# Expert stages of a hybrid model on one core: gathered and output rows as half rows on 128 partitions, transposes moved, block loops grouped

## The chip, the core and the metric

The kernel runs on one core of a Trainium2 chip. A core has TensorE (PE, matrix products and transposes into PSUM), VectorE (DVE), ScalarE (ACT), GpSimd (POOL) and SyncE (SP), and 16 DMA engines that move data between HBM and the core's SBUF. The metric is the device time of one execution in microseconds. All values are float32.

## The reference

`reference()` is two blocks. The first is a convolution module and a retention module on 512 tokens of width 1024. The second has two layers, each with windowed attention, local mixers, and a hierarchical mixture of experts. The mixture is the part that the change touches:

```python
N_EXPERTS, TOP_K, D_EXPERT = 32, 2, 512          # d_model 1024
expert = g_idx * EXP_PER_GROUP + e_idx           # two experts of one group for each token
...
xs = h[slot_tok].reshape(n_blocks, MOE_BLOCK, d_)
def run(args):
    xb, e = args
    return (jax.nn.silu(xb @ w1[e]) * (xb @ w3[e])) @ w2[e]
ys = lax.map(run, (xs, block_e)).reshape(-1, d_)
return jnp.zeros_like(h).at[slot_tok].add(ys * slot_gate[:, None])
```

Layer 0 routes 768 tokens (512 and a context of 256), layer 1 routes 512. Each expert has w1 and w3 of 1024x512 and w2 of 512x1024, 2 MiB each, so a layer reads 192 MiB of expert weights.

## The kernel before

The kernel is written by hand for each engine: every engine has its own instruction stream, and semaphores order them. Nothing reschedules them.

In an expert stage the tokens of each expert are packed into blocks of 64 slots (`SB`). The experts with even numbers form stream 0, those with odd numbers stream 1. A step `i` handles block `i` of stream 0 and then block `i` of stream 1 (`rounds`, L397). Each stream has one set of weight buffers (`m_w`), one of row buffers and four PSUM banks.

For block `i` of stream `s` TensorE runs `expert_step` (L1278): `products` (L1241: 8 k-steps, each with a product for w1 and one for w3, 64 columns of the array each, side by side, into one bank), then `turn_hidden` for block i-1 (L1254: four transposes of the gated hidden rows), `turn_rows` for block i+1 (L1230: eight transposes of the gathered rows, 64 partitions by 128), and `outputs` for block i-1 (L1265: w2, both halves of the columns side by side).

Around it, ScalarE applies SiLU (L854) and copies half of the output rows (L847). VectorE copies the transposed rows (L1895) and hidden rows (L1903) to SBUF, multiplies by the gate (L1921) and copies the other half of the output (L1911). GpSimd gathers the rows of block i+1 (indirect DMA, L2034, 64 rows of 4 KiB onto 64 partitions) and scatters those of block i-2 (L2050). SP loads the weights (`load_step`, L584, DMA at L575): w1 and w3 of block i+1 once `products` of block i of the same stream is done, w2 of block i once `outputs` of block i-1 is done. If block i+1 has the same expert as block i, a register makes the load a no-op.

The number of blocks is known only at run time. A fixed loop runs steps 2 to 15; a second loop (L405) runs over all remaining possible steps, 24 in layer 0 and 16 in layer 1, and each round asks whether `i <= last` (L406). `last` is the same for both streams: the longer one's last block. Every engine runs this loop.

Before the stage, products of one-hot matrices (L1218) turn the routing into slot lists: for each block the token rows and the gates, together in 128 output partitions. After the stage, the output rows are read back from HBM (L608) and the layer norm finishes on VectorE (L1950 to L1952).

## Time and profile before

| what | value |
|---|---|
| time, median of 3 runs (lowest to highest) | 3241.57 us (3236.73 to 3242.39) |
| the profiled execution's own time | 3238.72 us |
| its span, first to last instruction | 3236.9 us |
| TensorE busy | 2784.1 us (86%) |
| VectorE busy | 1128.3 us (35%) |
| DMA moved | 602.90 MB, 186 GB/s over the span |
| L1250 (`products`), x2688 | 658.5 us busy, 646 ns mean |
| L1273 (`outputs`), x1344 | 310.2 us busy, 603 ns mean |
| SiLU calls, L854 | x84 |

The page is one execution. Busy time of TensorE counts overlapping matmuls once. The 84 calls of L854 are the blocks that were computed in both layers, 42 steps of two streams. In the trace the first expert stage lies at about 1564 to 2175 us and the second at about 2544 to 3196 us. The granted clock (PEclk) is given as a share of full speed: 1.0 is 2.4 GHz, 0.5 is 1.2 GHz.

### The profile page before, as it was taken

The numbers are of one execution on the slowest core, as the hardware profiler recorded it, in microseconds if no ns is written. First come the engines' busy times: TensorE is split into PE (matmuls) and PEld (weight loads), VectorE is DVE, ScalarE is ACT, GpSimd is POOL, SyncE is SP. The second block draws the span as 40 slices with busy tenths as digits, with TensorE's granted clock in tenths as the row PEclk, the third lists the DMA queues.
The fourth block names the chain that finished last, engine by engine and source line by source line (L and its number), as shares of the span: only waits on it lengthen the run. The fifth ranks groups of instructions, "written<-read, shape, count | busy, mean of one in ns | idle before, by whom it ended". The sixth has DMA issues, their size and how long they took to land.

```text
span 3236.9 us, 33858 instructions
## 1 busy us (share of the span) xinstructions
PE 2784.1 (86%) x11728; PEld 1295.0 (40%) x11728; DVE 1128.3 (35%) x2173; ACT 458.6 (14%) x848; POOL 304.7 (9%) x432
## 2 busy tenths in 40 slices
PE   6999969999999999899698877866999679997783
PEld 3444424444444455555333322323564323332221
DVE  3998960320011232544511111127254411211114
ACT  2111131100110102521000000001151000100000
POOL 0101011000000000001211111110000211111110
PEclk9999989999999999998799989987989699998987
DMA  6655521222211201012699999974101798489994
GB/s 209 209 194 182 169 91 54 94 78 78 78 52 50 91 26 52 1 41 104 223 334 320 387 386 384 347 269 154 52 1 60 268 385 288 128 300 392 387 359 171
DMA packets 270442, 602.90 MB, mean 186 GB/s; under 512 B 18016, under 2 KB 42912, under 8 KB 268960
## 3 DMA queue, kind: packets, MB, share of 16 engines
q1 hardware_dynamic: 255584, 580.70, 49.8%
q0 software_dynamic: 14784, 21.21, 2.2%
q8 instruction: 47, 0.77, 0.1%
q14 instruction: 27, 0.22, 0.0%
HBM read 739.11 MB, written 29.46 MB: 237 GB/s over the span
## 4 chain that ended last, share of the span: by engine, by line
PE 70%; DMA 17%; DVE 6%; issue 3%; ACT 2%; SPq 1%; POOL 0%; DVEq 0%; POOLq 0%; ACTq 0%
DMA arena<-in_w 16%; PE psum L1250 14%; PE psum L916 10%; PE psum L965 10%; PE psum L1093 9%; PE psum L937 7%; PE psum L1188 4%; PE psum L1273 4%; PE psum L1140 2%; PE psum L1129 2%; PE psum L901 1%; SPq L575 1%; PE psum L986 1%; PE psum L1203 1%; PE psum L1152 1%
## 5 line engine op out<-in xcount | busy, mean ns | idle before, releaser
L1250 PE MATMUL psum<-arena 128*64 128x512 f32 x2688 | 658.5, 646 | 167.9 <-DMA arena<-in_w 123.4
L1250 PEld LDWEIGHTS psum<-arena 128*64 128x64 f32 x2688 | 221.2, 148 | 594.7 <-issue 549.3
L916 PE MATMUL psum<-arena 128*128 128x512 f32 x768 | 345.4, 603 | 2.8 <-ACT arena L647 2.8
L965 PE MATMUL psum<-arena 128*128 128x512 f32 x768 | 329.9, 592 | 0.8 <-ACT arena L639 0.8
L1273 PE MATMUL psum<-arena 128*64 128x512 f32 x1344 | 310.2, 603 | 16.6 <-DVE arena L1903 12.2
L1349 DVE SCALAR_TENSOR_TENSOR arena<-arena 128x512 f32<-128x512 f32 x464 | 308.7, 744 | 0.0
L1903 DVE COPY arena<-psum 128x256 f32<-128x256 f32 x84 | 35.5, 424 | 763.3 <-PE psum L1261 756.6
L1093 PE MATMUL psum<-arena 128*128 128x512 f32 (+1 forms) x800 | 288.3, 522 | 5.9 <-issue 4.0
L937 PE MATMUL psum<-arena 128*128 128x512 f32 x512 | 225.3, 603 | 11.1 <-POOL arena L1996 10.4
L965 PEld LDWEIGHTS psum<-arena 128*128 128x128 f32 x768 | 145.8, 190 | 184.2 <-issue 183.2
L916 PEld LDWEIGHTS psum<-arena 128*128 128x128 f32 x768 | 143.1, 191 | 175.0 <-issue 175.0
L1093 PEld LDWEIGHTS psum<-arena 128*128 128x128 f32 x800 | 152.9, 192 | 134.4 <-issue 124.7
L1273 PEld LDWEIGHTS psum<-arena 128*64 128x64 f32 x1344 | 100.1, 138 | 165.7 <-issue 165.7
L854 ACT ACTIVATE arena<-psum 64x512 f32<-64x512 f32 x84 | 49.9, 595 | 781.9 <-PE psum L1250 781.9
L937 PEld LDWEIGHTS psum<-arena 128*128 128x128 f32 x512 | 99.0, 194 | 137.1 <-issue 135.9
L1188 PE MATMUL psum<-arena 128*128 128x512 f32 x320 | 137.9, 593 | 3.3 <-ACT arena L803 3.3
L1911 DVE COPY arena<-psum 64x512 f32<-64x512 f32 x84 | 58.2, 693 | 219.4 <-PE psum L1273 219.4
L2011 POOL TENSOR_TENSOR arena<-arena 128x1024 f32<-128x1024 f32 x10 | 27.4, 2756 | 871.7 <-DVE arena L1517 871.7
L847 ACT ACTIVATE arena<-psum 64x512 f32<-64x512 f32 x84 | 49.6, 590 | 369.2 <-PE psum L1273 369.2
L2034 POOL DMA_INDIRECT arena<-moe_in,arena x88 | 91.4, 1039 | 78.9 <-POOL arena L2031 72.3
L2050 POOL DMA_INDIRECT moe_out<-arena x76 | 72.4, 952 | 235.6 <-DVE arena L1911 235.6
L1140 PE MATMUL psum<-arena 128*128 128x128 f32 x640 | 86.5, 287 | 9.4 <-issue 4.8
(268 smaller groups left out, 2144.9 us busy)
## 6 DMA issues: line engine op xcount, KB each, us to landing
arena<-in_w SPq DMA_DIRECT2D x260, 2048.0 KB
arena<-in_w_ada SPq DMA_DIRECT2D x48, 1024.0 KB, 5.2
arena<-in_conv_w_in SPq DMA_DIRECT2D x24, 1024.0 KB
arena<-in_ret_w_in SPq DMA_DIRECT2D x12, 2048.0 KB, 7.8
arena<-in_w_in SPq DMA_DIRECT2D x8, 2048.0 KB, 8.2
arena<-moe_out SPq DMA_DIRECT2D x10, 1024.0 KB, 9.0
arena<-in_conv_w_out SPq DMA_DIRECT2D x4, 2048.0 KB, 10.2
arena<-in_ret_w_out SPq DMA_DIRECT2D x4, 2048.0 KB, 7.9
```

The costliest lines, as they stand in the source:

```text
L916: m = pe.matmul(bank(b + c), w[:, k, c * P:(c + 1) * P], c_hT[:, k, :], start=(k == 0), stop=(k == KD - 1))
L937: m = pe.matmul(bank(2 * t + hf), mem(y + S * k + P * t, P), slot_rows(n)[:, k % 4, hf * CW:(hf + 1) * CW], start=(k == 0), stop=(k == KI ...
L965: m = pe.matmul(bank(4 * (n % 2) + j), l_, r_, start=(k == 0), stop=(k == KD - 1))
L1093: m = pe.matmul(o, l_, r_, start=(k == 0), stop=(k == KD - 1))
L1129: m = pe.matmul(psum[:, at:at + P * len(ts)], q, b_kT[part, h // 4, ts[0] * P:(ts[-1] + 1) * P], start=True, stop=True)
L1140: m = pe.matmul(bank(4 + kv, P, hh * P), b_sb[i % 2][:, 4 * kv + hh, c * P:(c + 1) * P], b_dg[i % 2][:, 4 * kv + hh, :], start=True, stop= ...
L1188: m = pe.matmul(bank(2 * (t % 4) + hf), y[:, t * P:(t + 1) * P], slot_rows(base + 4 + k // 4)[:, k % 4, hf * CW:(hf + 1) * CW], start=(k = ...
L1250: m = pe.matmul(bank(4 * s)[part], m_xsT[s][:, k, :], m_w[s][j][:, k, :], start=(k == 0), stop=(k == KD - 1))
L1273: m = pe.matmul(bank(4 * s + 3)[SB * hf:SB * hf + SB], m_hT[s][:, k, :], m_w[s][2][:, k, hf * CW:(hf + 1) * CW], start=(k == 0), stop=(k = ...
L1349: ins = dve.scalar_tensor_tensor(out=acc, in0=u, scalar=w[:, j:j + 1], in1=acc, op0=ALU.mult, op1=ALU.add)
L2034: pool.indirect_dma_start(out=m_xs[s], in_=moe_in[l], out_offset=None, in_offset=bass.IndirectOffsetOnAxis(m_gi[s], 0), bounds_check=nt * ...
L2050: pool.indirect_dma_start(out=moe_out[l], in_=m_y[s], in_offset=None, out_offset=bass.IndirectOffsetOnAxis(m_si[s], 0), bounds_check=2 * n ...
```

## The change

It has these parts.

1. **Half rows.** The HBM tensors of gathered and output rows are seen as rows of 512. One gather of a block brings 128 half rows of 2 KiB onto 128 partitions: partition p holds the first half of slot p's row, partition 64+p the second. The scatter writes 128 half rows. `m_xs` and `m_y` become 128x512. The rows' index lists have 128 entries per block, and the product that makes them (L1218) becomes two products, one for each half of the partitions; the gates get a product of their own.
2. **Four transposes.** `turn_rows` turns 128x128 tiles, four instead of eight per block.
3. **One bank pair per stream.** The transposed rows share a bank with the products of w1 and w3, and the transposed hidden rows share one with the outputs. `turn_rows` now waits until the gate multiplication has read the bank. `turn_hidden` moves into the middle of `products`, and `outputs` comes directly behind `products`, ahead of `turn_rows`.
4. **Copies.** The output rows need one ScalarE copy of 128x512 in place of one on ScalarE and one on VectorE. SiLU writes where the gate multiplication then works in place.
5. **Own last block per stream, in groups.** The second loop runs over groups of five steps; a group is skipped as a whole, and inside it each block of each stream has its own condition. Layer 0 has 5 groups, layer 1 has 4.
6. **Lookahead.** At the start of a stage only the rows of stream 0's first block are turned before the first product. The layer norm's scaling of residual rows (`complete_rows`) is put into two portions of six operations (layer 0) in place of four of three. w1 and w3 of a stream share one semaphore.

The core of the diff:

```diff
-            with eng.Fori(E // 2, NBS[l]) as i:
-                with eng.If(i <= last[0]):
-                    for s in range(2):
-                        step(s, i, first)
+            with eng.Fori(0, (NBS[l] - E // NS) // GROUP) as g:
+                with eng.If(g * GROUP + E // NS <= last[NS]):
+                    for j in range(GROUP):
+                        for s in range(NS):
+                            with eng.If(g * GROUP + (E // NS + j) <= last[s]):
+                                step(s, g * GROUP + (E // NS + j), first)
...
-                        m = pe.matmul(bank(6, nr), posw[:, j, :], blk[:, j, :], start=(j == 0), stop=(j == 2 * nt - 1))
+                        for hf in range(2):
+                            m = pe.matmul(bank(6, nr)[SB * hf:SB * hf + SB], row[:, j, :], blk[:, j, :],
+                                          start=(j == 0), stop=(j == 2 * nt - 1))
...
                     pe.wait_ge(moe(l, s, "gather"), count(l, s, "gather", 16 * i + 16))
                     if early >= 1:
-                        pe.wait_ge(moe(l, s, "rows"), count(l, s, "rows", i))
+                        pe.wait_ge(moe(l, s, "hidden"), count(l, s, "hidden", i))
                     pe.sem_inc(sem("settled"), 1)
-                    for k in range(KD):
-                        m = pe.transpose(bank(4 * s + 1, SB, SB * k), m_xs[s][:, k * P:(k + 1) * P],
-                                         ident[0:SB, 0:SB])
+                    for k in range(KD // 2):
+                        m = pe.transpose(bank(2 * s, P, P * k), m_xs[s][:, k * P:(k + 1) * P], ident)
...
                     for k in range(KD):
+                        at = P * (k % 4) + SB * (k // 4)
+                        if k == KD // 2 and early >= 1:
+                            turn_hidden(s, i - 1, early - 1)
...
                     products(s, i, early)
                     if early >= 1:
-                        turn_hidden(s, i - 1, early - 1)
+                        outputs(s, i - 1, early - 1)
+                    elif s + 1 < NS:
+                        turn_rows(s + 1, 0, 0)
                     turn_rows(s, i + 1, early + 1)
-                    if early >= 1:
-                        outputs(s, i - 1, early - 1)
-
-                for s in range(2):
-                    turn_rows(s, 0, 0)
+
+                turn_rows(0, 0, 0)
...
-                    act.activation(m_y[s][:, 0:CW], bank(4 * s + 3)[0:SB], ACT.Copy).then_inc(moe(l, s, "y"), 1)
+                    act.activation(m_y[s], bank(2 * s + 1), ACT.Copy).then_inc(moe(l, s, "y"), 1)
...
-                    pool.indirect_dma_start(out=m_xs[s], in_=moe_in[l], out_offset=None,
+                    pool.indirect_dma_start(out=m_xs[s], in_=halves_in, out_offset=None,
                                             in_offset=bass.IndirectOffsetOnAxis(m_gi[s], 0),
-                                            bounds_check=nt * P - 1, oob_is_err=False)\
+                                            bounds_check=2 * nt * P - 1, oob_is_err=False)\
```

The order of the instructions on TensorE in the fixed loop of layer 1, one block, before (products, hidden rows, gathered rows, outputs):

```order
L1250 MATMUL psum<-arena 64x512 x16
L1261 MATMUL psum<-arena 128x64 x4
L1232 ISA
L1237 MATMUL psum<-arena 128x64 x8
L1267 ISA
L1268 REGISTER_ALU
L1270 ISA
L1273 MATMUL psum<-arena 64x512 x8
```

and after the change (products L1295, hidden rows L1306, outputs L1317, gathered rows L1282):

```order
L1295 MATMUL psum<-arena 64x512 x8
L1301 REGISTER_ALU
L1303 REGISTER_ALU
L1306 MATMUL psum<-arena 128x64 x4
L1295 MATMUL psum<-arena 64x512 x8
L1312 ISA
L1313 REGISTER_ALU
L1317 MATMUL psum<-arena 64x512 x8
L1277 ISA
L1279 REGISTER_ALU
L1282 MATMUL psum<-arena 128x128 x4
```

The transposes of the hidden rows now split the products into two runs of eight, and the outputs follow without a transpose between. The other stream's block follows in the same order.

The second loop of layer 1 on TensorE, before, with its body of two blocks left out:

```order
L405 UNCONDITIONAL_BRANCH
L405 ISA
L406 COMPARE_AND_BRANCH
...
L406 UNCONDITIONAL_BRANCH
L405 REGISTER_ALU
L405 COMPARE_AND_BRANCH
```

and after the change, with the bodies left out:

```order
L436 UNCONDITIONAL_BRANCH
L436 ISA
L437 COMPARE_AND_BRANCH
L440 REGISTER_ALU
L440 COMPARE_AND_BRANCH
...
L440 UNCONDITIONAL_BRANCH
L440 REGISTER_ALU
L440 COMPARE_AND_BRANCH
...
L440 UNCONDITIONAL_BRANCH
L436 REGISTER_ALU
L436 COMPARE_AND_BRANCH
```

A skipped round took two branches for one step; now it takes two for five steps, and each block that is reached has a branch of its own.

The start of layer 1's expert stage on TensorE, before:

```order
L1237 MATMUL psum<-arena 128x64 x16
L1250 MATMUL psum<-arena 64x512 x16
L1237 MATMUL psum<-arena 128x64 x8
L1250 MATMUL psum<-arena 64x512 x16
L1237 MATMUL psum<-arena 128x64 x8
L1250 MATMUL psum<-arena 64x512 x16
L1261 MATMUL psum<-arena 128x64 x4
L1237 MATMUL psum<-arena 128x64 x8
L1273 MATMUL psum<-arena 64x512 x8
```

and after the change:

```order
L1282 MATMUL psum<-arena 128x128 x4
L1295 MATMUL psum<-arena 64x512 x16
L1282 MATMUL psum<-arena 128x128 x8
L1295 MATMUL psum<-arena 64x512 x16
L1282 MATMUL psum<-arena 128x128 x4
L1295 MATMUL psum<-arena 64x512 x8
L1306 MATMUL psum<-arena 128x64 x4
L1295 MATMUL psum<-arena 64x512 x8
L1317 MATMUL psum<-arena 64x512 x8
```

The second stream's rows are turned behind the first product and not ahead of it.

## Rows read from the trace of the kernel before

**Rows 1.** Windows of the two expert stages; columns as the first line says.
```profile
core 0: us, PE busy (x) PEld busy (x) DVE busy (x) ACT busy (x) POOL busy (x), PEclk, DMA share, GB/s
1668.00:1732.00 64.00, 61.39 (x328) 24.83 (x328) 14.04 (x23) 6.26 (x11) 12.69 (x23) 1.00 0.89 306
2113.00:2148.00 35.00, 34.04 (x180) 13.68 (x176) 7.18 (x12) 3.48 (x6) 3.69 (x8) 1.00 0.78 289
2692.00:2790.00 98.00, 92.81 (x480) 36.17 (x478) 19.57 (x32) 9.36 (x16) 18.16 (x32) 0.98 0.72 243
2790.00:2855.00 65.00, 64.00 (x342) 25.96 (x340) 14.67 (x24) 7.11 (x12) 12.87 (x24) 1.00 0.21 59
1803.00:2014.00 211.00, 163.84 (x760) 61.37 (x761) 29.46 (x48) 14.63 (x25) 27.24 (x48) 0.89 1.04 386
```

**Rows 2.** Chain in order of time (start us, us, what), two blocks bound by TensorE.
```profile
2783.61 6.87 PE psum L1250 x32
2790.48 0.39 PE psum L1261 x4
2790.87 0.50 PE psum L1237 x8
2791.38 0.15 issue
2791.52 3.65 PE psum L1273 x16
2802.56 0.43 DVE arena L1903
```

**Rows 3.** The same view, end of the first expert stage.
```profile
2143.80 3.65 PE psum L1273 x16
2147.45 11.72 issue
2160.63 9.36 PE psum L1273 x32
```

**Rows 4.** Line L406: branches of the skipping loop on TensorE's queue.
```profile
L406 PEldq COMPARE_BRANCH  x40: 73/213/215, 2031.4 to 3178.3; - x40
```

**Rows 5.** Chain, before the router: transposes of 128x128.
```profile
1510.82 1.75 PE psum L1027 x8
1512.57 3.26 PE psum L1203 x16
```

**Rows 6.** Page, part 5: SiLU on ScalarE.
```profile
L854 ACT ACTIVATE arena<-psum 64x512 f32<-64x512 f32 x84 | 49.9, 595 | 781.9 <-PE psum L1250 781.9
```

**Rows 7.** Chain at the second stage's first weight load.
```profile
2559.62 8.39 DMA arena<-in_w
2568.02 5.58 issue
```

**Rows 8.** Chain, end of the second expert stage.
```profile
3146.86 0.39 PE psum L1261 x4
3163.15 6.87 PE psum L1250 x32
```

**Rows 9.** Timeline, end of the second stage (start us, us, engine, line, operation).
```profile
3182.82 8.54 PE L1273 MATMUL psum<-arena 128*64 128x512 f32 x32 [2.66 <-DVE arena L1903]
```

**Rows 10.** Timeline, start of the first expert stage.
```profile
1582.22 1.21 DVE L1933 TENSOR_TENSOR arena<-arena 128x1024 f32<-128x1024 f32 x1
```

**Rows 11.** Page, part 3: the indirect DMAs' queue (packets, MB, share).
```profile
q0 software_dynamic: 14784, 21.21, 2.2%
```

**Rows 12.** Indirect DMAs' queue in 1563 to 1580 us.
```profile
q0 software_dynamic: 320, 0.86, 18.1%
```

**Rows 13.** Page, part 5: the gathers' issue on GpSimd.
```profile
L2034 POOL DMA_INDIRECT arena<-moe_in,arena x88 | 91.4, 1039 | 78.9 <-POOL arena L2031 72.3
```

**Rows 14.** Lines L916 and L901, the program's first loop, four rounds.
```profile
L916 PE MATMUL psum<-arena x768: 592/592/1192, 32.5 to 421.6; 128*128 128x512 f32 x192
L901 PE MATMUL psum<-arena x1536: 272/273/298, 42.6 to 423.0; 128*32 128x128 f32 x192
```

More of the change, by code:

```diff
@@ L45 @@
 SB = 64
+NS = 2
+EPN = -(-E // NS)
+GROUP = 5
 NO_ROW = 4096
@@ L381, in build @@
-        REUSED0 = [
-            {"index": ("ra_ms", 4), "turned": ("ri_mm", 48), "rows": ("ri_dve", 16)},
-            {"index": ("ra_sd", 4), "turned": ("ri_act", 32), "rows": ("ra_sc", 16)}]
+        MOE_SEMS = ("w13", "w2", "gather", "scatter", "index", "turned", "rows", "product", "silu", "hidden",
+                    "hid_t", "hid_rows", "out", "y")
+        U = T + TX
+        reused_hw = [("const_in", 32), ("ctx_in", 32), ("fg_in", 16), ("x_in", 16 * TX), ("cv_w0", 192), ("cv_w1", 192)]
@@ new lines, in build @@
+        reused_late += [("kT", 2 * T), ("kt", 2 * T), ("at_o", 4 * U), ("ob_x", 2 * U), ("ob_mm", 2 * U), ("lg_mm", U),
+                        ("upad", 2), ("rt_M", 2), ("rt_act", 4), ("rt_dve", 4), ("at_l", AH * U), ("at_s", AH * U),
+                        ("at_p", AH * U), ("at_e", (AH + 1) * U)]
+        REUSED = [{}, {}]
+        for s_ in range(NS):
+            for what_ in MOE_SEMS:
+                if what_ in ("w13", "w2"):
+                    REUSED[1][s_, what_] = reused_hw.pop()
+                elif what_ in ("gather", "scatter"):
+                    if reused_pool:
+                        REUSED[1][s_, what_] = reused_pool.pop()
+                else:
+                    REUSED[1][s_, what_] = reused_late.pop() if reused_late else reused_old.pop()
@@ L385, in shared @@
+        for s_ in range(NS):
+            for what_ in MOE_SEMS[4:]:
+                if reused_old:
+                    REUSED[0][s_, what_] = reused_old.pop()
         def shared(l, s, what):
-            return (REUSED if l else REUSED0)[s].get(what, (f"m{s}_{what}", 0))
+            return REUSED[l].get((s, what), (f"m{s}_{what}" if what in MOE_SEMS[:2] or l == 0 else f"n{s}_{what}", 0))
         def moe(l, s, what):
@@ L567, in _ @@
                 sp.wait_ge(sem("hx2_out"), past("hx2_out", l) + 16 * nt)
-                for j, what in enumerate(("w1", "w3", "w2")):
-                    sp.dma_start(m_w[1][j], ws[j][:, kk[j]:2 * kk[j], :]).then_inc(moe(l, 1, what), 16)
+                for j in range(3):
+                    first_weights(1, j)
                 sp.wait_ge(sem("meta"), past("meta", l) + 1)
@@ L1213, in _ @@
                 nr = NR[l]
-                posw, blk = mem3(g_posw, 2 * nt, 2 * SB), mem3(g_blk, 2 * nt, nr)
+                row, wgt, blk = (mem3(o, 2 * nt, n) for o, n in ((g_row, SB), (g_wgt, SB), (g_blk, nr)))
                 for k in range(2):
@@ L1223, in _ @@
                                      ident[0:nr, 0:nr])
+                m.then_inc(sem("rank"), 1)
+                for j in range(2 * nt):
+                    m = pe.matmul(bank(5, nr, 256)[0:SB], wgt[:, j, :], blk[:, j, :], start=(j == 0),
+                                  stop=(j == 2 * nt - 1))
                 m.then_inc(sem("rank"), 1)
@@ L2015, in _ @@
                 pool.wait_ge(sem("hx_in"), past("hx_in", l) + nt)
-                for s in range(2):
+                for s in range(NS):
                     link(pool.memset(m_xs[s], 0.0))
@@ L2061, in _ @@
-                for s in range(2):
-                    gather(s, 0, 0)
+                    gather(s, i + 2, early + 2, 2 * i + 2 if early >= 1 else 3)
+                    if early >= 1:
+                        scatter(s, i - 1, early - 1, 2 * i + 3)
+                for s in range(NS):
+                    gather(s, 0, 0, 1)
+                for s in range(NS):
+                    gather(s, 1, 1, 2)
                 pool.wait_ge(sem("meta"), past("meta", l) + 1)
                 last = last_blocks(pool, l)
-                rounds(pool, l, last, move_step, first=3)
@@ L2079, in _ @@
-                for s in range(2):
+                rounds(pool, l, last, move_step)
+                for s in range(NS):
+                    scatter(s, last[s], 1, 2 * last[s] + 4)
+                for s in range(NS):
                     pool.wait_ge(moe(l, s, "scatter"), count(l, s, "scatter", 16 * last[s] + 16))
                     settled()
-                    pool.wait_ge(moe(l, s, "gather"), count(l, s, "gather", 16 * last[s] + 32))
+                    pool.wait_ge(moe(l, s, "gather"), count(l, s, "gather", 16 * last[s] + 48))
```

280 lines of the change are left out of this document (132 added, 148 removed).

## The prediction

> **What bounds the kernel now.** Only the two expert stages change, so I read them alone, by stretches. The windows [rows 1] show two regimes. From 1803 to 2014 us the DMA engines are full (share 1.04, 386 GB/s) while TensorE is busy 164 of 211 us: there a step of two blocks waits for its weights, and nothing that TensorE does faster or slower counts. In four other stretches TensorE is busy 95 to 98% of the time and the DMA share is 0.89, 0.78, 0.72 and 0.21: the blocks there reuse an expert's weights, and TensorE sets the pace. They last 64 + 35 + 98 + 65 = 262 us. The chain of waits in one of them [rows 2] gives the block: 6.87 us products, 0.39 us four hidden transposes, 0.50 us eight row transposes, 0.15 us until the outputs start, 3.65 us outputs, 11.56 us in all. So the 262 us hold about 22.6 blocks. Every second block also has VectorE's copy of the hidden rows (0.43 us, the last of rows 2) on the path, which takes the place of the row transposes and costs about the same.
>
> The third thing to see is idle time at the ends. In the first stage TensorE finishes block 18's outputs at 2143.80 + 3.65 = 2147.45 us and then does nothing for 11.72 us [rows 3]: 20 rounds of the second loop are skipped, 0.586 us each. A branch on its queue takes 213 ns [rows 4], and a skipped round has two. The outputs of the last blocks then take 9.36 us, at a clock that has fallen, for what takes 2 x 3.65 at 2.4 GHz.
>
> **The change part by part.** Which blocks exist follows from the inputs: with the reference's routing the streams have 20 and 20 blocks in layer 0 and 21 and 22 in layer 1. The kernel before computes 2 x 20 + 2 x 22 = 84, the changed one 83.
>
> *The block on TensorE.* The three transposing pieces cost 0.39 + 0.50 + 0.15 = 1.04 us for 12 transposes of 64-partition tiles. The eight alone take 0.50, so 0.0625 us each, and 12 x 0.0625 = 0.75; the other 0.29 us are two changes of tile shape, from the products' 128x64 tiles to the transposes' and back. After the change four transposes stand inside the products: 0.25 + 0.29 = 0.54 us. The four row transposes are 128x128. Eight of these took 1.75 us [rows 5], so four take 0.88, with two more changes of shape 1.17 us. Together 1.71 in place of 1.04, or +0.67; VectorE's copy no longer waited for gives back some 0.1. I take +0.55 us a block. The lowest this can be is -0.3 (transposes of 128x128 at the price of two small ones, and no cost at the extra changes of shape, since rows 5 show none between two groups of 128x128 tiles), the highest +1.0 (the whole 0.29 at each of two extra changes, and 0.22 us a transpose). The new wait, `turn_rows` for the gate multiplication, is hidden: SiLU takes 595 ns [rows 6], the multiplication works on a tile of the same size, and the outputs, 3.65 us, lie in front.
> 22 blocks x 0.55 = +12 us (bounds -7 and +22).
> The Trainium skill, TensorEngine Tiling (Array Packing), Key Properties, says that changing the tiling mode, and not just the tile, drains TensorE. The 0.15 us between the last transpose and the outputs [rows 2] agrees. By that rule four changes a block in place of two would be the larger part of the loss, and the sum would stay as it stands; what it speaks against is the lower bound.
>
> *End of the first stage.* The outputs of block 18 end about 0.5 us earlier (outputs before row transposes, one insertion more), at 2147. Skipping costs four groups of 0.586 and two single branches with their arithmetic, 0.3 each: 2.9 us. The last hidden transposes follow to about 2151.5. w2 of the last block is issued when block 18's outputs end. From issue to the next product a fresh pair w1, w3 took 8.39 + 5.58 = 14.0 us [rows 7]; 4.2 MB at 386 GB/s are 10.9 of these, so w2 with half the bytes takes 14.0 - 5.4 = 8.6 us, until 2155.6. Stream 0's outputs run before, stream 1's until 2159.3, against 2169.99 before. -10.5 us. What is late next is w2's load. Bounds: -12 (clock up, load quicker) and -3 (a branch inside a group as dear as a whole round).
>
> *End of the second stage.* Block 21 of stream 0 goes, 11.56 us of TensorE, but its expert's neighbour is waited for: w1 and w3 of block 21 of stream 1 are issued when product (1,20) ends, at 3146.86 [rows 8], and land 14.0 us later at 3160.9, against a product that started at 3163.15. So only 2 us come of the block that is gone. The product then ends at 3168.9, the outputs of block 20 at 3172.5, w2 lands 8.6 us later at 3181.1, and the last outputs end at 3184.8, against 3182.82 + 8.54 = 3191.36 [rows 8, 9]. -6, after half a microsecond for the lower clock. Bounds -9 and -2. The skipping (eight single branches, two groups, 3.6 us in place of 10 rounds) lies beside the load.
>
> *Start of a stage.* One row turn and the wait for the second gather leave the path to the first product, -1.3 us in each layer. Against that the second product waits for the gate multiplication and then for the row turns (+2.1), and in layer 0 VectorE's six scalings in a row, 1.2 us each [rows 10], hold back a hidden copy (+2). The split products for the slot lists run as side-by-side halves, 24 pairs, at about the time of 24 whole ones. Together +0.5 for both layers, bounds -3 and +6 (the pairs not side by side: twice 5.4 us in layer 0, partly beside VectorE).
>
> *Indirect DMAs.* The queue took 2.2% of the span for 21.21 MB [rows 11], 71 us of all 16 engines. In 1563 to 1580 us it shows 320 packets with 0.86 MB in 18.1% of 17 us x 16 [rows 12], so 0.86 MB are about 210 rows of 4 KiB at 230 ns, and the rest are unused slots and completions. The bytes stay, the rows double. If the half row costs half, nothing changes; if each adds 20 ns, 5120 more rows are 6 us of all engines, and half of the stages' time is full. GpSimd's issue took 1039 ns for 64 rows [rows 13]; 128 may take up to twice that, which is beside TensorE's 11.6 us except for the first gather and the last scatter of a stage. I take +1 (bounds -4 and +7).
>
> Sum: +12 - 10.5 - 6 + 0.5 + 1 = -3 us. The profiled execution took 3238.72 us (span 3236.9), so 3235.7; that execution lies 2.85 us under the median of 3241.57, and I set the time against the median: 3238.6, say 3239.
>
> **The rivals.**
> *The transposes cost nothing on the path.* For it: the queue of weight loads in front of a block in the 0.89 and 0.78 stretches absorbs a late product, and rows 5 show no pause at a change of instruction. Against: 0.21 in the 65 us stretch, where nothing absorbs. The 12 us fall to 0 or below: 3239 - 13 = 3226.
> *The block costs 1.0 us more or TensorE counts in more blocks.* For it: rows 2 show every gap on the chain, and the product that starts when its weights land is also 0.54 us longer, which in a stretch that is nearly full delays the next load. 32 blocks x 0.95 = 30 us in place of 12: 3239 + 18 = 3257, slower than before. It decides from about 0.7 us a block in 22 blocks, or 0.55 in 29. Against: in the full stretches TensorE has 47 us of idle time in 12 or 13 blocks, nearly 4 us each.
> *The groups' code must be fetched again.* A group on TensorE is ten blocks of 60 pairs of weight load and matmul, 1200 instructions and some 150 others. If it did not stay loaded, each of the six skipped groups would wait for code twice, at 2 to 3 us: about 30 us, of which the w2 loads hide half: 3239 + 15 = 3254. Against: the first loop of the program has (768 + 1536) / 4 = 576 pairs a round [rows 14], 1152 instructions, and it runs on from 32.5 to 423 us with matmuls of 592 and 272 ns and no wait on code that I can see. The Trainium skill, Runtime: NRT & Kernel Launch, Instruction fetch mechanics, gives TensorE 2048 instructions of memory and the other engines 512; by it TensorE's group would fit. On the others a group is some 230 instructions or fewer.
> *The change does not do what it says*, that is, the end wait stays since another engine leaves the loop later: VectorE left it last in layer 1 (the last outputs waited 2.66 us for its copy [rows 9]). The ends would give -8 in place of -16.5: 3247.
>
> **How the numbers follow.** Forecast, 3239 with its own range 3230 to 3248: 0.45. Transposes free, 3226: 0.2. Dear blocks, 3257: 0.17. Code fetched again: 0.06. Ends half won: 0.12. A measurement of this kernel can tell about 0.2%, 6.5 us, from no change: faster is below 3235, slower above 3248. The forecast's 0.45 splits 0.14, 0.28, 0.03; the second gives 0.18 faster and 0.02 same; the third and fourth 0.21 slower and 0.02 same; the last 0.07 same, 0.05 slower. Faster 0.32, same 0.39, slower 0.29. The range 3225 to 3257 leaves 0.2 out.
>
> **What the profile after would show.** Right: blocks of 12.0 to 12.3 us in the stretch that reuses weights in layer 1, with row transposes of 0.9 us; no 11.72 us of idle TensorE in layer 0 but 3 to 5; 83 SiLU calls; in layer 1 a wait for weights ahead of the last product; the same 34 us steps where the DMA share is 1.04. Wrong: a block of 11.5 us or less, or above 12.6; steps in the full stretches that change by more than 0.5 us, which would put the half rows in the DMA engines at fault; idle TensorE at a branch in the middle of the second loop.

## The result

| | before | after |
|---|---|---|
| median | 3239.32 us (3236.73 to 3242.39, 4 runs) | 3218.06 us (3211.45 to 3222.34, 4 runs) |
| profiled execution, span | 3238.72, 3236.9 us | 3222.34, 3220.5 us |

The ratio of the times is 0.9932, with a 95% interval of 0.991 to 0.9954: 21 us faster, below the predicted range (3225 to 3257). The profiled execution is the slowest of the four, so its trace shows 16 us of the 21.

**The pace of TensorE.** The chain of waits in the stretch of layer 1 that reuses weights ([rows 2] show the same for before; L1306 are the hidden rows' transposes, L1295 the products, L1317 the outputs, L1282 the gathered rows' transposes):

```profile
2764.51 0.39 PE psum L1306 x4
2764.90 3.58 PE psum L1295 x16
2768.49 3.43 PE psum L1317 x16
2771.92 0.59 PE psum L1282 x4
2772.51 3.58 PE psum L1295 x16
2776.09 0.39 PE psum L1306 x4
```

From one set of hidden transposes (L1306) to the next are 11.58 us, against 11.56 before. No pause stands between the pieces. Four transposes of 128x128 (L1282) take 0.59 us.

**The full stretch**, with the columns of rows 1 (TensorE busy, its weight loads, VectorE, ScalarE, GpSimd, granted clock, DMA share, GB/s):

```profile
1803.00:2014.00 211.00, 169.55 (x728) 59.23 (x724) 24.08 (x39) 15.49 (x26) 29.62 (x49) 0.90 1.04 393
```

The DMA share is 1.04 as before, but 393 GB/s are moved in place of 386 [rows 1]. From the end of the first product to the end of the last, layer 0 takes 557.6 us against 562.6 before, layer 1 takes 606.0 against 610.7, the latter with a block fewer. (Here and below, where a time is given from the end of a product without a row, the end is read from the start of the SiLU that waits for it, 0.13 us later.)

**The end of layer 0.** The chain, without its short pieces:

```profile
2132.45 3.58 PE psum L1295 x16
2136.03 3.43 PE psum L1317 x16
2139.46 0.60 PE psum L1282 x4
...
2144.02 0.43 DVE arena L1950
2144.59 8.62 PE psum L1317 x32
```

The last outputs end at 2153.21 us, 17.18 us after the last product. Before, that was 27.14 us, 11.72 of them idle [rows 3]. Between the row transposes (L1282) and VectorE's copy (L1950) are 4 us, nearly all of them VectorE's own branches. TensorE was out of the loop earlier: it is idle for 2.16 us and has ended the last hidden transposes at 2143.04 us.

**The end of layer 1.** The last product ends at 3147.14 us. What follows on the chain is SP's queue (SPq), which no row of before shows:

```profile
3143.56 3.58 PE psum L1295 x16
3147.14 3.46 PE psum L1317 x15
3150.92 0.39 SPq L615
...
3153.16 4.45 issue
3157.74 3.54 issue
3161.35 2.23 issue
3163.62 2.94 issue
3166.70 2.83 issue
3169.60 2.00 issue
3171.64 2.98 issue
3174.82 0.36 SPq L571
...
3176.77 7.48 DMA arena<-moe_out
3184.37 1.24 DVE arena L1987
```

L615 at 3150.92 us is SP's last load of weights, L571 its first one behind the loop. Between them SP has nothing to wait for, and yet it leaves the loop only at 3174.82 us. TensorE's last outputs had ended at 3165.6 us, 18.4 us after the last product. From the last product to the first operation on the output rows (L1987) are 37.2 us, against 30.7 before.

Page, part 3 and part 5: the indirect DMAs' queue, queue 14, which carries instructions (27 packets before), and SiLU, 83 calls in place of 84:

```profile
q0 software_dynamic: 14944, 21.23, 1.9%
q14 instruction: 51, 0.41, 0.0%
L893 ACT ACTIVATE arena<-psum 64x512 f32<-64x512 f32 x83 | 49.3, 595 | 875.2 <-PE psum L1295 875.2
```

### The profile page after: what moved, and what is told of

The parts are those of the page before. It is cut to its first block, busy times and chain, and to the rows that moved or that the text cites. A ratio compares the mean times of both kernels' runs of the same rounds, so it can differ in the third digit from the quotient of the medians.

```text
span 3220.5 us, 33096 instructions
## 1 busy us (share of the span) xinstructions
PE 2781.2 (86%) x11400; PEld 1265.5 (39%) x11400; DVE 1076.8 (33%) x2088; ACT 458.2 (14%) x846; POOL 315.7 (10%) x436
## 4 chain that ended last, share of the span: by engine, by line
PE 69%; DMA 19%; DVE 6%; issue 3%; ACT 2%; SPq 1%; POOL 0%; DVEq 0%; POOLq 0%; ACTq 0%
DMA arena<-in_w 18%; PE psum L1295 14%; PE psum L955 10%; PE psum L1004 10%; PE psum L1132 9%; PE psum L976 7%; PE psum L1227 4%; PE psum L1317 3%; PE psum L1179 2%; PE psum L1168 2%; PE psum L940 1%; PE psum L1025 1%; PE psum L1242 1%; SPq L615 1%; PE psum L1191 1%
## 5 line engine op out<-in xcount | busy, mean ns | idle before, releaser
L1295 PE MATMUL psum<-arena 128*64 128x512 f32 x2656 | 672.9, 653 | 169.2 <-DMA arena<-in_w 167.4
L1295 PEld LDWEIGHTS psum<-arena 128*64 128x64 f32 x2656 | 205.0, 148 | 515.7 <-issue 510.4
L1317 PE MATMUL psum<-arena 128*64 128x512 f32 x1328 | 303.3, 600 | 3.6 <-DVE arena L1950 2.8
L1950 DVE COPY arena<-psum 128x256 f32<-128x256 f32 x83 | 35.1, 424 | 490.9 <-PE psum L1306 484.6
L893 ACT ACTIVATE arena<-psum 64x512 f32<-64x512 f32 x83 | 49.3, 595 | 875.2 <-PE psum L1295 875.2
L1317 PEld LDWEIGHTS psum<-arena 128*64 128x64 f32 x1328 | 97.0, 139 | 195.2 <-issue 195.2
L1960 DVE SCALAR_TENSOR_TENSOR arena<-arena,psum 64x512 f32<-64x512 f32 x83 | 61.3, 739 | 327.4 <-ACT arena L893 327.4
L1943 DVE COPY arena<-psum 128x512 f32<-128x512 f32 x87 | 60.1, 691 | 211.9 <-PE psum L1282 211.9
L2070 POOL COPY arena<-arena 128x1 int32 (+1 forms) x91 | 17.8, 196 | 878.8 <-PE psum L1282 837.5
L1179 PE MATMUL psum<-arena 128*128 128x128 f32 x640 | 86.5, 287 | 9.4 <-issue 4.8
## 6 DMA issues: line engine op xcount, KB each, us to landing
arena<-moe_out SPq DMA_DIRECT2D x10, 1024.0 KB, 10.5
```

Source lines behind the costliest of these rows:

```text
L1179: m = pe.matmul(bank(4 + kv, P, hh * P), b_sb[i % 2][:, 4 * kv + hh, c * P:(c + 1) * P], b_dg[i % 2][:, 4 * kv + hh, :], start=True, stop= ...
L1295: m = pe.matmul(bank(2 * s)[part], m_xsT[s][:, at:at + SB], m_w[s][j][:, k, :], start=(k == 0), stop=(k == KD - 1))
L1317: m = pe.matmul(bank(2 * s + 1)[SB * hf:SB * hf + SB], m_hT[s][:, k, :], m_w[s][2][:, k, hf * CW:(hf + 1) * CW], start=(k == 0), stop=(k = ...
L1960: dve.scalar_tensor_tensor(out=m_h[s], in0=m_h[s], scalar=gate, in1=bank(2 * s)[0:SB], op0=ALU.mult, op1=ALU.mult).then_inc(moe(l, s, "hid ...
```

## The experiments

All times are medians. The kernels of one group ran beside the kernel before on the same chip. The ratios are to it.

### First group: what does SP cost, and which half rows pay?

**The changed kernel again.** No edit.

> The changed kernel as it is, for comparison with the three kernels run beside it. Both theories: 0.993 of the kernel before, about 3218 us, with steps of 33.2 us in the stretch of layer 1 where the DMA engines are full, and 7 us in the trace's chain of waits on SP between the last outputs of layer 1 and the reading of the output rows.

Measured: 3216.99 us (3214.54 to 3218.88), ratio 0.9934 (0.9921 to 0.9946). SP is ready (it issues L571, its first load behind the loop) 27.7 us after the last product of layer 1, and the read of the output rows is issued at 29.45 us.

**SP in single steps.**

```diff
-                rounds(sp, l, last, load_step)
+                rounds(sp, l, last, load_step, group=1)
```

> SP alone runs the second loop in single steps (as the kernel before did), the other engines keep groups of five. Theory: in layer 1 SP leaves its last group late, because each jump over a block that is left out lands on instructions that must be fetched (waits of 2 to 4.5 us each in the changed kernel's chain from 3151 to 3175 us); a single step stays loaded. The reading of the output rows then starts at the landing of the last scatter, about 7 us earlier than now: 3211 us, 0.998 of the changed kernel, with no SP issue on the chain there. Rival: SP is not late by itself but ends when the last scatter and the signal for it arrive, or what GpSimd does is as late: same time as the changed kernel within 2 us, the chain there then shows GpSimd. A second rival: single steps cost SP two branches for each of 14 skipped rounds, 0.3 to 0.6 us each, so 4 to 8 us, and nothing is won.

Measured: 3208.6 us, ratio 0.9904 (0.989 to 0.9919). SP is ready 11.47 us after the last product, and the read is issued at 21.15 us, at the landing of the last scatter:

```profile
3166.26 2.27 DMA moe_out<-arena
...
3168.84 5.68 DMA arena<-moe_out
```

The theory's main claim holds: 8 us of SP's late exit were on the path. In layer 0 the single steps cost something. SP takes 10.5 us there for 22 rounds (2135.0 to 2145.5 us) in place of 2.9 for five, issues the loads behind the loop later, and the last scatter lands after 6.85 us in place of 2.62. That the scatter is slow because of these loads is argued, not shown.

**Gathers of whole rows**, on 64 partitions:

```diff
-        m_xs = [mem(W0 + 12288 + 512 * s, CW) for s in range(NS)]
+        m_xs = [mem(W0 + 2048 + D * s, D, SB) for s in range(NS)]
...
-                    for k in range(KD // 2):
-                        m = pe.transpose(bank(2 * s, P, P * k), m_xs[s][:, k * P:(k + 1) * P], ident)
+                    for k in range(KD):
+                        m = pe.transpose(bank(2 * s, SB, SB * k), m_xs[s][:, k * P:(k + 1) * P],
+                                         ident[0:SB, 0:SB])
```

> Only the gathers go back to whole rows of 4 KiB on 64 partitions, with eight transposes of 64x128 a block; the scatters stay half rows. Theory one (the gathered half rows on 128 partitions load the DMA engines less): the steps in the full stretch of layer 1 go back from 33.2 to 33.7 us, and the time rises by 8 to 10 us over both layers, to 3227 us. Theory two (the scatters do it, or the order of the products does): steps stay at 33.2 us and the time stays within 3 us of the changed kernel's. On the block bound by TensorE both say the same: the transposes take 0.50 us and their change 0.15 us in place of 0.59, so 22 blocks are 0 to 2 us longer.

Measured: 3243.06 us, ratio 1.0013 (1.0005 to 1.0022). It is theory one, but 26 us and not 8 to 10. The block bound by TensorE is 11.63 us. The rest stands in the windows of the full stretches, of this kernel:

```profile
1850.00:2000.00 150.00, 118.81 (x530) 42.52 (x532) 16.01 (x26) 10.12 (x17) 19.32 (x33) 0.89 1.04 386
```

and of the changed kernel:

```profile
1850.00:2000.00 150.00, 118.26 (x506) 42.00 (x504) 16.71 (x27) 10.72 (x18) 22.01 (x36) 0.91 1.04 393
```

In the stretches ahead of it the steps are longer too. From the end of the first product to that of the seventh this kernel takes 73.15 us in layer 0, the changed kernel 67.92 and 69.17 in its two profiled executions (this group's and that of the result); in layer 1 these are 85.18 against 82.42 and 83.00.

**Scatters of whole rows**, from 64 partitions:

```diff
-                    act.activation(m_y[s], bank(2 * s + 1), ACT.Copy).then_inc(moe(l, s, "y"), 1)
+                    for hf in range(2):
+                        act.activation(m_y[s][:, CW * hf:CW * (hf + 1)], bank(2 * s + 1)[SB * hf:SB * (hf + 1)], ACT.Copy)\
+                            .then_inc(moe(l, s, "y"), 1)
```

> Only the scatters go back to whole rows of 4 KiB from 64 partitions (two ScalarE copies of 64x512 a block in place of one of 128x512); the gathers stay half rows. Theory one (the gathers make the full steps shorter): steps stay at 33.2 us, the time within 3 us of the changed kernel's. Theory two (the scatters do): steps of 33.7 us, 8 to 10 us longer. If neither this kernel nor the one with whole gathers moves the steps, the half rows are not the cause and the order of TensorE's work is. Both: the last copy of a stage is 0.6 us later on ScalarE, twice, 1 us.

Measured: 3215.15 us, ratio 0.9934 (0.992 to 0.9948), 394 GB/s in the same window. The scatters' shape is worth nothing that the runs can tell.

### Second group: length or partitions, and the parts of the order

**Half rows, two gathers onto the same 64 partitions** (the second with `element_offset=CW`, transposes as with whole rows):

```diff
+                    for hf in range(2):
+                        pool.indirect_dma_start(out=m_xs[s][:, CW * hf:CW * (hf + 1)], in_=halves_in, out_offset=None,
+                                                in_offset=bass.IndirectOffsetOnAxis(m_gi[s], 0),
+                                                element_offset=CW * hf,
```

> The rows are gathered as half rows of 2 KiB, but onto 64 partitions: two gathers of 64 half rows a block, side by side in the free dimension, and eight transposes of 64x128, as in the kernel with whole gathers. Theory one (what costs is the length of the row: 4 KiB pieces among the weights' own of about 2 KiB): as the changed kernel, 3217 us, steps of 33.5 us in the full stretch, and 388 to 393 GB/s there. Theory two (what costs is that all rows land on 64 of the 128 partitions): as the kernel with whole gathers, 3243 us, steps of 34 us or more, 359 to 386 GB/s in stretches whose DMA share is over 1. Both: GpSimd has one issue of 1 us more a block, which is beside the 11.6 us of a block.

Measured: 3248.46 us, ratio 1.0028 (1.0019 to 1.0038). Theory two, and 5 us more than with whole rows, with twice the issues. Halving the row's length wins nothing as long as the rows land on 64 partitions. The DMA view of 2058 to 2085 us gives GB/s in 40 slices of 0.675 us. The changed kernel (first group), the one with whole gathers, and this one:

```profile
GB/s 416 395 407 388 388 385 382 388 388 388 385 391 385 383 352 385 388 380 401 382 388 385 385 385 388 391 391 410 407 401 419 413 413 397 343 391 401 394 391 404
```

```profile
GB/s 404 373 397 361 206 231 234 294 370 404 407 401 413 394 428 413 407 401 385 419 279 282 361 400 410 385 413 388 388 388 388 388 388 385 385 382 388 385 388 388
```

```profile
GB/s 385 391 267 325 261 246 346 407 380 416 413 400 401 425 407 413 382 388 401 264 397 276 370 388 397 404 401 407 379 388 388 388 388 385 382 391 382 388 385 385
```

In the second and third the rate falls to 206 to 330 GB/s for some four slices at a time, with the engines counted as busy throughout; in the first it never leaves 343 to 419. The stretches 1850 to 1877, 1900 to 1927 and 1950 to 1977 us say the same: there the slices of the kernel before and of these two fall to 212 to 325 GB/s again and again, those of the changed kernel never below 361. Over the four slices 206, 231, 234, 294 the loss against 388 is about 1 us. That one kernel has the dips and the other has not is shown; why they arise is not. The Trainium skill, SBUF — State Buffer, Door 1: The DMA port swizzle, says that partitions 0 to 63 reach only 8 of the 16 ports by which DMA writes SBUF. The trace agrees in the dips to nearly half of 388. No run here tried other sets of 64 partitions, and in the kernels with the dips the gathered rows also lie at another address within a partition than in the changed one; no run moved them alone. Reading from 64 partitions (the scatters above) showed nothing of the kind.

**Hidden rows turned behind the products:**

```diff
-                        if k == KD // 2 and early >= 1:
-                            turn_hidden(s, i - 1, early - 1)
...
                     if early >= 1:
+                        turn_hidden(s, i - 1, early - 1)
                         outputs(s, i - 1, early - 1)
```

> The transposes of the hidden rows stand behind the sixteen product pairs, ahead of the outputs, and not in their middle; all else as changed. Theory: the insertion costs nothing and hides VectorE's copy of the hidden rows (0.43 us) and TensorE's wait for it. Without it the outputs wait: a block bound by TensorE grows from 11.58 to about 12.0 us, 22 blocks are 10 us, 3227 us in all. Rival (my prediction's: each change of instruction shape costs 0.15 us, and the insertion brings two more): the block shrinks by 0.3 and grows by 0.43, so it stays within 0.15 us and the time within 3 us. In the full stretches both say no change: 33.5 us steps.

Measured: 3223.31 us, ratio 0.9949 (0.9934 to 0.9964), 5 to 6 us more than the changed kernel. The chain in the stretch that reuses weights:

```profile
2763.86 0.39 PE psum L1304 x4
2764.25 0.56 issue
2764.81 3.65 PE psum L1315 x16
2768.47 0.59 PE psum L1282 x4
2769.05 7.02 PE psum L1293 x32
2776.07 0.40 PE psum L1304 x4
```

A block is 12.21 us, as the theory said and more than the rival allowed: 0.56 us of waiting for VectorE's copy come back. The two changes of shape that the insertion brings cost 7.16 - 7.02 = 0.14 us together at most, and the copy that it hides is four times that. The time rises by half of the theory's 10 us: from the first product to the last, layer 1 is 7.2 us longer than in the changed kernel of the first group (611.87 against 604.69), layer 0 no longer (550.43 against 550.92).

**The common last block:**

```diff
-            return [eng.value_load(g_n[l][0:1, s:s + 1], min_val=E // NS - 2, max_val=NBS[l] - 2) + 1
-                    for s in range(NS + 1)]
+            v = eng.value_load(g_n[l][0:1, NS:NS + 1], min_val=E // NS - 2, max_val=NBS[l] - 2) + 1
+            return [v] * (NS + 1)
```

> Both streams again run to the last block of the longer one, groups of five kept. Layer 0 has 20 and 20 blocks and does not change. In layer 1 block 21 of stream 0 is computed again (84 blocks). Theory: of its 11.56 us of TensorE nearly all lies beside the load of w1 and w3 of the other stream's block 21, as in the kernel before, so 0 to +3 us: 3218 us. Rival: the block's own load of 6 MB (a gathered block without rows has an expert too) or its place ahead of the last block puts 10 us or more on the path: 3228 us.

Measured: 3205.77 us (3203.43 to 3206.29), ratio 0.9891 (0.9873 to 0.9909). Neither theory said that: 11 us faster with one block more. Block 21 itself costs little: from the end of layer 1's first product to the end of its last are 607.39 us, against 604.69 and 605.99 in the changed kernel's two profiled executions. These 1.4 to 2.7 us are no clear cost, since kernels without block 21 show 602.6 to 608.7. But SP is ready 15.2 us after the last product in place of 27.7, and the read is at 22.25 us, 7 us earlier. In the profiled executions another 4 us lie in the attention of layer 1, which nobody touched. The windows of the changed kernel (first) and of this one:

```profile
2330.00:2340.00 10.00, 8.34 (x32) 5.69 (x29) 5.64 (x18) 4.76 (x11) 0.00 (x0) 0.50 0.00 0
```

```profile
2330.00:2340.00 10.00, 7.41 (x44) 5.18 (x43) 7.24 (x23) 7.35 (x17) 0.00 (x0) 0.99 0.00 1
```

TensorE's granted clock is 0.50 (1.2 GHz) in one and 0.99 (2.4 GHz) in the other, after the same work; a group of eight products there (L1168) takes 2.09 us in the first and 1.14 us in the second. The kernel with SP in single steps shows 1.00, and the changed kernel of the result 0.94. When the clock falls is not what the edit is about.

**Single steps on all engines** (`GROUP = 1`):

> No groups: every engine runs the second loop in single steps, 24 rounds in layer 0 and 16 in layer 1 as before, each block with its own condition. Theory (skipping is what the 10 us at the end of layer 0 were): TensorE is idle again for 20 rounds of about 0.6 us in layer 0, +8 us there; in layer 1 SP is no longer late (-8 us) and 10 rounds on VectorE and TensorE take 6 us in place of 3 (+3): 3221 us, between the changed kernel (3217) and before (3240). Rival: the gain at the end of layer 0 comes from the outputs being ahead of the row transposes and not from skipping: then 3210 us.

Measured: 3218.67 us, ratio 0.9933 (0.9917 to 0.9948). This is the theory's 3221 and not the rival's 3210. At the end of layer 0 the skipping is back:

```profile
2135.24 0.59 PE psum L1282 x4
2135.83 13.67 issue
```

In layer 1 SP is ready 9.4 us after the last product. So the groups won 11 us in layer 0 by skipping fewer rounds and lost 8 of them on SP in layer 1.

### Third group: the groups, and why SP is late

**Both cures for SP**, single steps on SP and the common last block:

> SP in single steps and both streams to the common last block. If each of the two removes its own 8 to 11 us, 3197 us. Theory: both remove the same thing, SP's late leaving of the second loop in layer 1 (in the trace of the kernel with single steps SP is ready 11.5 us after the last product, with the common last block 15.2 us, in the changed kernel 27.7 us, and the output rows could be read from 21 us on): 3206 us, no better than the kernel with the common last block alone (3205.8). Block 21 of stream 0 stays free of cost since the last weights land later than it ends.

Measured: 3209.19 us (3202.46 to 3215.48), ratio 0.9913 (0.9898 to 0.9927). As the theory said, the two remove the same thing: together they are no faster than either alone.

**The kernel before with groups of four**, nothing else:

```diff
-            with eng.Fori(E // 2, NBS[l]) as i:
-                with eng.If(i <= last[0]):
-                    for s in range(2):
-                        step(s, i, first)
+            with eng.Fori(0, (NBS[l] - E // 2) // 4) as g:
+                with eng.If(g * 4 + E // 2 <= last[0]):
+                    for j in range(4):
+                        with eng.If(g * 4 + (E // 2 + j) <= last[0]):
+                            for s in range(2):
+                                step(s, g * 4 + (E // 2 + j), first)
```

> The kernel before with groups of four in the second loop (24 and 16 rounds as before, no other part of the change). Theory: the part that skipping plays is 10 to 11 us at the end of layer 0 (11.72 us of idle TensorE become about 2) and 1 to 3 us at the end of layer 1, unless SP leaves late there: 3228 us, 0.996 of before. Rival: the end of layer 0 got shorter by the new order (outputs ahead of the row transposes, w2 asked for earlier) and groups alone give 5 us or less: 3235 us or more.

Measured: 3226.64 us, ratio 0.9958 (0.9945 to 0.9972), 12.5 us less than before, as the theory said. From the last product of layer 0 to the end of TensorE's outputs 18.0 us, from 27.1.

**Groups of eight**, SP in single steps (`GROUP = 8`):

> Groups of eight steps on TensorE, VectorE, ScalarE and GpSimd, SP in single steps. A group on TensorE is sixteen blocks of 32 + 16 + 4 + 4 matmuls and as many weight loads, about 1900 to 2000 instructions with branches, in place of 1200. Theory: TensorE keeps its code (the changed kernel's groups show 2.2 to 2.4 us for leaving the loop, no more than its branches), so the time is within 4 us of the kernel with single steps on SP (3208.6), a few branches fewer. Rival (my third in the prediction: the groups' code is fetched again): at this size it does not stay loaded, TensorE waits 2 to 3 us for each jump over a block or group, and the time is 10 us or more above, 3219 us.

Measured: 3227.52 us, ratio 0.9966 (0.9953 to 0.9979), 19 us more than with groups of five and SP in single steps (3208.6). The rival. The chain at the end of layer 0 and of layer 1:

```profile
2136.57 19.52 issue
...
3166.97 10.82 issue
```

TensorE takes 19.52 and 10.82 us to leave the loop. In layer 0 it passes twelve branches there (eight blocks, and two groups with two each). The changed kernel has ten in layer 0 and twelve in layer 1, and TensorE passes them in 2.16 and 2.39 us. The branches are of the same kind; what differs is the length of the body. Its queue shows single branches that take microseconds, in this kernel (first two lines, layer 0) and not in the changed one (third):

```profile
L440 PEldq COMPARE_BRANCH  x6: 207/1562/5669, 2135.2 to 2147.9; - x6
L436 PEldq COMPARE_BRANCH  x3: 83/221/6093, 2148.2 to 2155.7; - x3
L436 PEldq COMPARE_BRANCH  x5: 83/221/224, 2138.7 to 2141.8; - x5
```

In these 19.52 us (2136 to 2156) queue 8, the other queue of instructions, moves five packets of 16 KB. While the changed kernel leaves its loops, it moves one in layer 0 (2136 to 2143) and none in layer 1 (3150 to 3154).

**SP's loop shifted:**

```diff
+                if l == 1:
+                    for _ in range(40):
+                        sp.sem_inc(sem("settled"), 1)
                 rounds(sp, l, last, load_step)
```

> The changed kernel with 40 increments of an unused semaphore in SP's stream ahead of layer 1's block loop. They take 1 to 3 us while SP waits for a product anyway, and shift the code of the loop. Theory (SP's wait at the end of layer 1 is code being fetched at both ends of the second loop, and whether both ends stay loaded depends on where they lie): the wait can go away, SP is then ready 10 to 15 us after the last product and not 27.7, and the time is 3209 us; if it stays, another shift would be needed. Rival (the wait belongs to the length of the group alone, or to the register arithmetic of separate last blocks): as the changed kernel, 3217 us, SP ready 27 us after the last product.

Measured: 3208.85 us (3207.01 to 3211.06), ratio 0.9908 (0.9895 to 0.9921): 40 idle instructions more, and 8 us less. SP's instructions of line L436 (the loop's end and head), in layer 1 of the profiled changed kernel and of this one (durations in ns, first and last start in us):

```profile
L436 SPq ALU_OP  x3: 33/33/33, 3157.6 to 3174.6; - x3
```

```profile
L436 SPq ALU_OP  x3: 33/33/33, 3148.6 to 3150.0; - x3
```

From the end of the first of these three rounds to the end of the third are 17.0 us in one and 1.4 us in the other. In layer 0 the changed kernel's SP has five in 2.9 us (2140.7 to 2143.6). The group is as long and the arithmetic the same in both kernels, so neither makes the wait by itself; where the loop lies decides. That the wait is for code, the DMA queues show. In the changed kernel from 3147 to 3175 us:

```profile
q14 instruction: 11, 0.09, 1.1%
```

In the shifted one, from 3142 to 3170 us, queue 14 has no packet, and over the whole execution it has 35 in place of 51. The Trainium skill, Runtime: NRT & Kernel Launch, Instruction fetch mechanics, says that an engine other than TensorE holds two blocks of 256 instructions (TensorE 2048 instructions) and must fetch when a branch is taken out of what it holds. That agrees with a loop of about 280 instructions whose end and head alternate, each 2 to 4.5 us, and with TensorE's groups of eight. Only one shift was tried.

## Why the prediction was wrong

**The forecast was too slow by 21 us. The block on TensorE was priced 12 us too high, and the gathers on 128 partitions were priced at +1 where going back to 64 costs 26.** SP's late end in layer 1, which was not foreseen, hid part of the gain. My first rival, "The transposes cost nothing on the path", gave 3226 and was the nearest. It was right on the block (11.58 us) and says nothing of the gathers.

*The block on TensorE (+12 us, measured 0).* The step that failed is "Eight of these took 1.75 us [rows 5], so four take 0.88, with two more changes of shape 1.17 us". Rows 5 were taken at half clock. The windows of before around them:

```profile
1500.00:1507.00 7.00, 3.43 (x20) 2.11 (x18) 5.22 (x13) 2.06 (x7) 0.00 (x0) 0.96 0.58 191
1507.00:1512.00 5.00, 4.78 (x23) 4.81 (x24) 2.23 (x7) 1.04 (x3) 0.00 (x0) 0.50 1.03 389
```

At 2.4 GHz four take 0.59 us. The second half of the step, 0.29 us for each pair of changes of shape, came from subtracting eight transposes from twelve. Half of it, the 0.15 us until the outputs start, was a wait for VectorE's copy: with the insertion undone that wait is 0.56 us, and two changes of shape show at most 0.14. The rule of the Trainium skill that I had weighed, TensorEngine Tiling (Array Packing), Key Properties, is not borne out at that size. Against before, the products take 0.29 us more (7.16 against 6.87) and the row transposes 0.09 more, the outputs take 0.22 less (3.43 against 3.65) and the 0.15 us of waiting are gone: 11.58 against 11.56 us. Why the products and the outputs shift against each other is not shown.

*Indirect DMAs (+1, bounds -4 and +7; measured -26 in the changed kernel).* This term was mis-sized most, and with its sign. I priced the rows by bytes and by their own time in the queue: "The bytes stay, the rows double". The queue's share did fall, from 2.2 to 1.9%, but 0.3% of the span is 10 us of all engines and not 26. A gather onto 64 partitions costs the rate of the weights that run beside it, which the queue's row can't show. It was to be seen in the trace of before, in slices finer than a step (the same view, 2058 to 2085 us):

```profile
GB/s 215 276 376 388 388 395 407 385 388 388 407 410 413 400 419 352 267 364 407 379 385 404 407 407 385 385 388 382 391 385 388 385 392 310 382 388 388 388 388 380
```

"Steps in the full stretches that change by more than 0.5 us" was my sign for a wrong prediction. Most did: from SiLU to SiLU of one stream, the middle one of the full steps takes 34.3 us before and 33.9 and 33.6 after in layer 0, 34.0 before and 33.1 and 33.3 after in layer 1.

*End of the first stage (-10.5, measured -10.0).* The idle time and its cure were read rightly; that the size is right is partly luck. What was late next was not w2's load, for which TensorE does not wait at all. It was the branches, 4 us on VectorE, and then the outputs of both streams, which run in one piece of 8.62 us (granted clock 0.65 in their first 4.4 us, 1.00 after).

*End of the second stage (-6, measured +6.5 from the last product to L1987 in the profiled runs).* The block that goes is worth 1.4 to 2.7 us by the traces, not clear of their scatter, where I had 2. The wait for weights ahead of the last product is there. The rest failed in three places. TensorE's outputs end 18.4 us after the last product and not 15.9 (3168.9 to 3184.8 in my working, where the terms add up to 3168.3 for the first), and by another path: I had one stream's outputs behind w2's load, but 5 us of transposes, branches and VectorE's copy come behind block 20's outputs, and then both streams' outputs in 9.97 us (clock 0.50 in the first 5.4 us). SP then issues the read at 3176.77 us, about 7 us after the last scatter could have been read. The read takes 7.48 us, and 4.86 before. For SP the failing step is one sentence: "On the others a group is some 230 instructions or fewer". I had asked for TensorE whether the code would have to be fetched again, and answered right (groups of five leave in 2.2 to 2.4 us). The trace records 27 or 28 instructions of SP for a block, so about 280 for a group, and I did not ask where its loop's two ends lie.

*Start of the stages (+0.5, bounds -3 and +6).* The first product of layer 0 ended 1.8 us earlier than before in one profiled execution and 4.2 in the other, measured from the start of the program, so with the scatter of all that lies ahead. The first step behind it is 3.7 us longer in layer 0 (19.0 against 15.3 us from SiLU to SiLU of stream 0) and 0.8 to 1.2 in layer 1. The parts of this term were not tested one by one.

*The sum.* With the terms as measured, the 3239 become 3239 - 12 (block) + 0.5 (end of layer 0) + 12.5 (end of layer 1) - 27 (gathers) - 3 (start) = 3210, and the kernel takes 3217 to 3218. The 7 or 8 us that are missing come, as far as the runs show, from adding: the 26 us of the gathers are counted in the changed kernel, where whole gathers hurt more than in the kernel before. From the end of the first product to that of the seventh the kernel with whole gathers takes 73.15 us in layer 0 (66.55 before, 67.92 changed in the first group) and 85.18 in layer 1 (82.05 before, 82.42 changed), 9.7 us more than before in both. With less lookahead a slow gather is waited for; that is argued from the order of the work, and no run tried the lookahead by itself.

*The rivals.* "Dear blocks" fails by the 11.58 us. "Fetched again" is false on TensorE at ten blocks, true at sixteen, and true on SP. "The change does not do what it says" came true in layer 1 by another engine than the one I named: SP, not VectorE. VectorE is the last of the computing engines out of the loop in layer 0, 1 us behind TensorE.

*The faster versions.* SP in single steps, SP shifted, or the common last block each give 3206 to 3209 us, 0.989 to 0.991 of before. Between them the runs can't choose. Groups on SP in layer 0 and single steps in layer 1, where SP's rounds take 2.9 and 7.2 us, were not tried.

## What to carry to other kernels

Read the granted clock beside every duration that is moved to another stretch; eight transposes that took 1.75 us at half clock take 1.18 at full (twice the 0.59 of four). Judge a small DMA by what it does to the large ones beside it, in slices of under 1 us, and spread its rows over all 128 partitions. When a loop body is grown to skip faster, count the instructions of every engine's body and look at the engine that has nothing to wait for at the end.

## What the hardware showed that was not expected

- Beside weight loads that fill the DMA engines, a gather onto 64 partitions takes the rate of all DMA from 388 to between 206 and 330 GB/s for 1 to 3 us. Shorter rows (2 in place of 4 KiB) do not help (3248 and 3243 us), and scatters from 64 partitions cost nothing (3215 against 3217 us).
- A jump in SP's loop costs 2 to 4.5 us, or about 0.35 (two rounds of two jumps in 1.4 us), by the position of the loop in its stream. 40 idle instructions ahead of it save 8 us.
- TensorE leaves a loop with a body of ten blocks in 2.2 to 2.4 us of idle time and one of sixteen blocks in 19.52 and 10.82 us; single branches take up to 6.1 us there in layer 0, against 0.2.
- The stretch of attention in layer 1 from the first L1168 to the first L1179 takes 16.1 us in the changed kernel and 11.7 in the one with the common last block, with nothing changed there, when the granted clock is 0.50 in place of 0.99 from 2330 to 2340 us.
